# A hybrid decoder trunk with product-key experts: TensorE's weighted sum of v rows as 64x64 diagonal blocks, two slots at a time

## The chip, the cores and the metric

One Trainium2 chip, one core. The time is device microseconds for one execution of the whole program. Engines are called TensorE (PE; its weight loads PEld), VectorE (DVE), ScalarE (ACT), GpSimd (POOL) and SyncE (SP).

## The reference

Two layers on 512 tokens of width 1024, all in float32. Each layer first mixes tokens (norm, one input projection, a differential-attention group and a gated-linear-attention group, an output projection, residual). Then comes the part that takes most of the time, the retrieval of experts:

```python
def block(xb):                                   # 128 tokens
    q = (xb @ w_q).reshape(tb, 8, 2, 128)
    s = jnp.einsum('thcd,hckd->thck', q, sub_keys)
    top_s, top_i = lax.top_k(s, 16)
    ...
    u = u_tab[expert]                            # (128, 8, 16, 1024)
    act = jax.nn.gelu(jnp.einsum('td,thkd->thk', xb, u))
    w = gate * act
    return jnp.einsum('thk,thkd->td', w, v_tab[expert])
```

For each token, head and one of 16 picks, a row of 1024 floats comes from the table u and one from the table v: 2 layers x 512 tokens x 8 heads x 16 picks x 2 rows x 4 KB, 1.07 GB. The last line, the sum of v rows weighted by w, is what the change is about.

## The kernel before

**Units of work.** A tile is 128 tokens, one to a partition. A chunk is one head of one tile, 16 slots; a slot is one pick. There are 64 chunks, 1024 slots. For each slot GpSimd issues two indirect DMAs of 128 rows (`gather`, L464 to L471): a u row for each partition into `u_ring`, a v row into `v_ring`. Each ring has 6 buffers of 128x1024. GpSimd's order is fixed (L479 to L490): the u gather of slot s of chunk c+1, then the v gather of slot s of chunk c. A u gather waits until the slot six earlier is used (`u_used`), a v gather likewise (`v_used` if TensorE summed that slot, `v_added` if VectorE did).

**A slot's arithmetic.** VectorE multiplies the u rows with the tokens' h and sums over the row (`slot_u`, L986), a dot product for each partition. When the 16 dots of a chunk are there, ScalarE takes their gelu (`begin`, L659) and VectorE multiplies with the gates (L979): the 16 weights of a token. Then the v rows are summed. Of 16 slots VectorE takes slots 7 and 15 (`by_vector`), one scalar_tensor_tensor each onto `xs`, the residual (L996). TensorE takes the other 14: ScalarE writes a 128x128 diagonal matrix with the slot's weights (L669, from the identity, four buffers `diag`), and TensorE multiplies it with the v rows in two products of 128x512 that accumulate in PSUM (`slot_v`, L1257 to L1261). A float32 product stands in the trace as two MATMUL and two LDWEIGHTS instructions. `peer_acc` is 128x1024, two of eight PSUM banks. After the 8 chunks of a tile VectorE adds it to `xs` in one instruction (`add_tile`, L968 to L972), and TensorE's next tile waits for that (`peer_added`).

**Fronts.** All else (norms, projections, attention, the linear part, output projection, queries, top-k) is a front: 4 of them, each for 2 tiles of a layer. Each engine's program of a front is a generator that yields after each small part; 136 parts make a front, the last 40 of them routing. The first front runs alone up to part 101; from then on `interleave` (L338) puts parts between slots: each slot runs `slot_u` of the next chunk, then the front's parts that have come due (a front's parts spread over 256 slots, 10 ahead), then `slot_v`. So on TensorE the products of the next front (L1045, L1132, L1146, L1154) lie between the v slots, on VectorE its top-k and norms between the u products. From about 2772 us on there is no front left. Queues are in order on every engine: a wait holds all that stands behind it.

**Banks.** The six other PSUM banks carry the fronts' products. TensorE takes them in rotation, three for those that ScalarE empties (`fill_act`, L1009) and three for those that VectorE empties (`fill_dve`, L1015), and waits until the bank's last content is out. The order in which ScalarE and VectorE empty them is computed from the parts' positions (L136 to L153).

**Loads.** SyncE issues the weights, 2 MB at a time into two buffers, and the other inputs.

```python
for s in range(SLOTS):
    if c + 1 < CHUNKS:
        ...
        gather(u_rows, u_ring, U_RING, u_landed, c + 1, s)
    if c >= 0:
        ...
        pool.wait_ge(v_added if by_vector(old_s) else v_used, v_count(old_c, old_s))
        gather(v_rows, v_ring, V_RING, v_landed, c, s)
```

Of the kernel before, what the change touches and what calls it, by code (L numbers as in the profile page):

```python
# [22 lines left out]
P = 128  # L23
# [9 lines left out]
DIAGS = 4  # L33
ACT_BANKS = 3
DVE_BANKS = 3
V_EVERY = 8
LEAD = 10

# [15 lines left out]
def trunk(nc, x, attn_norm_w, w_in, q_norm_w, k_norm_w, lq1, lk1, lq2, lk2, diff_norm_w, gate_w2, gate_b,  # L54
# [40 lines left out]
    LR_AT = QK_AT + 4  # L95
    ATTN_AT = QK_FLIP_AT + HALF + 1
    ATTN_STEP = 5
    ATTN_STEPS = HALF * HEADS // 2
    GLA_AT = (LR_AT + 2, LR_AT + 16)
    FINISH_AT = (ATTN_AT + 14, ATTN_AT + 24)  # L100
# [35 lines left out]
    groups = [(2 * g, 0, "proj") for g in range(PROJ * HALF)] + [(LR_AT, 1, "lr")]  # L136
    groups += [(QK_FLIP_AT + i, 2, "qkT") for i in tiles for _ in range(2)]
    groups += [(ATTN_AT + ATTN_STEP * (s + 1), 3, "aT") for s in range(ATTN_STEPS) for _ in range(2)]
    groups += [(GLA_AT[i] + p, 4 + i, "gla") for i in tiles for p in (4, 4, 7)]
    groups += [(MIX_AT[i], 6, "mixT") for i in tiles for _ in range(2)]  # L140
    groups += [(STATS_AT[i] + 2, 7, "h2T") for i in tiles for _ in range(2)]
    groups += [(QUERY_AT, 0, "route"), (QUERY_AT + 2, 1, "route")]
    act_order = ["hT"] * 2 * HALF + [name for _, _, name in sorted(groups)] + ["route"] * (QS * QJ - 2)
# [34 lines left out]
    with ExitStack() as ctx:  # L178
        def sb(name, shape, dt=F32):
            return ctx.enter_context(nc.sbuf_tensor(name, shape, dt))  # L180
# [93 lines left out]
        wts = sb("wts", [P, 2, SLOTS])  # L274
        diag = sb("diag", [P, DIAGS, P])


        peer_acc = ctx.enter_context(nc.psum_tensor("peer_acc", [P, D], F32))
        act_bank = [ctx.enter_context(nc.psum_tensor(f"act_bank{i}", [P, 512], F32)) for i in range(ACT_BANKS)]
# [49 lines left out]
        def by_vector(s):  # L329

            return s % V_EVERY == V_EVERY - 1

# [96 lines left out]
        def _(pool):  # L429
# [10 lines left out]
            link(pool.memset(ident[:], 0.0))  # L440
            keep(ident[:], ALU.not_equal, 0, 1, [[-1, P]], 1.0)
            link(pool.memset(eps_c[:], EPS))
            link(pool.memset(one_c[:], 1.0))
# [50 lines left out]
        def _(act):  # L494
# [30 lines left out]
            def front(k):  # L525
# [11 lines left out]
                for p in range(MID_STEPS):  # L537
# [13 lines left out]
                    for _ in range(PRODUCT_PARTS[p]):  # L551
                        yield
                    if p == QUERY_AT + 3:
                        empty(scores[:, 0, 0])
                    if p == LR_AT + 1:
                        empty(lrT[0:RANK, :], HTOK, RANK)
                    i = p - QK_FLIP_AT - 1
                    if 0 <= i < HALF:
                        empty(qT[:, :, i * P:(i + 1) * P])
                        empty(kT[:, :, (t0 + i) * P:(t0 + i + 1) * P])  # L560
# [100 lines left out]
            def slot_v(c, s):  # L661
                if s == 0:
                    act.wait_ge(wts_ready, c + 1)
                if by_vector(s):
                    return
                n = v_count(c, s) - 1
                if n >= DIAGS:
                    act.wait_ge(v_used, n - DIAGS + 1)
                nc.scalar.activation(diag[:, n % DIAGS, :], ident[:], ACT.Copy,  # L669
                                     scale=wts[:, c % 2, s:s + 1]).then_inc(diag_ready, 1)  # L670
# [5 lines left out]
        def _(dve):  # L676
# [291 lines left out]
            def add_tile(tile):  # L968

                dve.wait_ge(v_used, (tile + 1) * PH * V_PE)  # L970
                v = xs[:, tile % TILES, :]
                tell(nc.vector.tensor_tensor(v, v, peer_acc[:], ALU.add), peer_added, "peer_added")  # L972

# [31 lines left out]
        def _(pe):  # L1005
# [45 lines left out]
            def front(k):  # L1051
# [8 lines left out]
                for p in range(MID_STEPS):  # L1060
# [26 lines left out]
                    if p == LR_AT:  # L1087
# [5 lines left out]
                        ins.then_inc(act_filled, 1)  # L1093
                    i = p - QK_FLIP_AT
                    if 0 <= i < HALF:
                        pe.wait_ge(qk_ready, k * HALF + i + 1)
                        for j in range(2):
                            flip([dqk[:, i, j * QH + h * P:j * QH + (h + 1) * P] for h in range(HEADS)])
# [3 lines left out]
                    for i in range(HALF):  # L1102
                        if p == MIX_AT[i]:
                            pe.wait_ge(mix_ready, k * HALF + i + 1)
                            flip_tile(mix[:, i, :])
                        if p == QUERY_AT + 2 and i == 0:
                            pe.wait_ge(keys_loaded, 16 * (l + 1))
                            pe.wait_ge(act_emptied, emptied(k, "route", 1))
                            score(0, 0)
# [136 lines left out]
            def slot_v(c, s):  # L1246
                if by_vector(s):
                    return
                tile, head = divmod(c, PH)
                n = c * SLOTS + s  # L1250
                e = head * TOPK + s
                last = head == PH - 1 and v_count(c, s) == (c + 1) * V_PE
                if e == 0 and tile > 0:
                    pe.wait_ge(peer_added, tile)
                pe.wait_ge(v_landed[n % V_RING], 16 * (n // V_RING + 1))
                pe.wait_ge(diag_ready, v_count(c, s))
                for j in range(D // 512):  # L1257
                    ins = nc.tensor.matmul(peer_acc[:, j * 512:(j + 1) * 512], diag[:, (v_count(c, s) - 1) % DIAGS, :],  # L1258
                                           v_ring[:, n % V_RING, j * 512:(j + 1) * 512],
                                           start=(e == 0), stop=last)  # L1260
                ins.then_inc(v_used, 1)  # L1261

# [31 lines left out]
```

## Time and profile before

| | |
|---|---|
| median of 3 runs | 3348.75 us (3347.01 to 3353.49) |
| span of the profiled execution | 3366.8 us (its own time beyond the span is not recorded) |
| instructions | 25897 |
| busy: TensorE, VectorE, ScalarE, GpSimd | 79%, 68%, 22%, 67% of the span |
| mean granted TensorE clock | 0.927 of full |
| first gather issued | 225.7 us |
| DMA | 1185 MB, mean 352 GB/s |

The profile is of one execution. Its time stands 18 us above the median of the runs, so differences are taken against it and then carried to the median. A wait row names the instruction that waited and what ended the wait; the time an engine is idle before an instruction costs something only if that engine is what others wait for. The DMA share of a stretch is the mean busy share of 16 DMA engines and can be a little over 1.

### The profile page before, as it was taken

How to read it: one execution, taken by the hardware profiler on the slowest of the kernel's cores; microseconds unless marked ns; L12 is line 12 of the kernel's file. 1: busy time of each engine (PE TensorE's matmuls, PEld its weight loads, DVE VectorE, ACT ScalarE, POOL GpSimd, SP SyncE). 2: the span in 40 equal slices, each digit the busy share in tenths (PEclk: the TensorE clock that was granted, in tenths of full speed). 3: DMA queues.
4: the chain of work that ended last, by engine and by line, in shares of the span. 5: the costliest groups of instructions: out<-in, count | busy, mean ns of one | idle time of the engine just before them, and what ended most of it. 6: DMA issues, size and time to landing. Idle time of an engine off the chain costs nothing.

```text
span 3366.8 us, 25897 instructions
## 1 busy us (share of the span) xinstructions
PE 2658.0 (79%) x7200; PEld 1257.8 (37%) x7200; DVE 2274.4 (68%) x4952; ACT 737.2 (22%) x1644; POOL 2267.3 (67%) x2074
## 2 busy tenths in 40 slices
PE   7866778998888778987887868998888776666667
PEld 3444333444354333433344423334435332222222
DVE  1559964579579984668659994568758995455443
ACT  2411121223221121223221121223322111111111
POOL 0025677777766777777776677777776676777776
PEclk9888899999998899999999889999999898988989
DMA  5248999999999999999999899999999999999998
GB/s 185 75 172 301 345 345 408 406 405 368 361 388 351 379 341 400 407 407 362 350 396 381 325 361 384 405 406 393 358 389 368 335 328 350 346 370 371 368 362 332
DMA packets 351442, 1185.41 MB, mean 352 GB/s; under 512 B 37666, under 2 KB 38212, under 8 KB 351044
## 3 DMA queue, kind: packets, MB, share of 16 engines
q0 software_dynamic: 294912, 1073.87, 84.2%
q1 hardware_dynamic: 56388, 109.88, 8.9%
q8 instruction: 60, 0.98, 0.1%
q14 instruction: 82, 0.67, 0.1%
HBM read 1181.52 MB, written 2.10 MB: 352 GB/s over the span
## 4 chain that ended last, share of the span: by engine, by line
POOL 27%; PE 23%; DVE 20%; issue 17%; DMA 11%; another core or an unknown queue 1%; ACT 1%; DVEq 0%; POOLq 0%; ACTq 0%
POOL v_ring L468 13%; POOL u_ring L468 13%; PE peer_acc L1258 12%; DMA v_ring<-in_peer_v,experts 8%; PE act_bank L1045 5%; DVE u_ring L986 4%; DMA u_ring<-in_peer_u,experts 4%; PE dve_bank L1045 2%; DVE work L752 2%; DVE work L741 1%; DVE work L749 1%; DVE work L738 1%; DVE work L931 1%; DVE work L933 1%
## 5 line engine op out<-in xcount | busy, mean ns | idle before, releaser
L1258 PE MATMUL peer_acc<-v_ring,diag 128*128 128x512 f32 x3584 | 1805.4, 645 | 647.1 <-DMA v_ring<-in_peer_v,experts 296.7
L986 DVE SCALAR_TENSOR_TENSOR u_ring<-u_ring,h 128x1024 f32<-128x1024 f32 x1024 | 1255.2, 1226 | 841.2 <-DMA u_ring<-in_peer_u,experts 730.1
L468 POOL DMA_INDIRECT v_ring<-in_peer_v,experts x1024 | 1146.9, 1120 | 524.3 <-issue 259.6
L468 POOL DMA_INDIRECT u_ring<-in_peer_u,experts x1024 | 1114.9, 1089 | 561.2 <-issue 308.9
L1258 PEld LDWEIGHTS peer_acc<-v_ring,diag 128*128 128x128 f32 x3584 | 688.5, 203 | 1647.7 <-issue 1009.4
L669 ACT ACTIVATE diag<-ident,wts 128x128 f32<-128x128 f32 x896 | 325.8, 397 | 1180.5 <-PE peer_acc L1258 580.9
L1045 PE MATMUL act_bank<-w_ring,hT 128*128 128x512 f32 x768 | 346.4, 598 | 0.7 <-ACT hT L508 0.7
L1045 PEld LDWEIGHTS act_bank<-w_ring,hT 128*128 128x128 f32 x768 | 147.5, 193 | 187.0 <-issue 185.6
L996 DVE SCALAR_TENSOR_TENSOR xs<-v_ring,wts,xs 128x1024 f32<-128x1024 f32 x128 | 164.5, 1285 | 49.5 <-DMA v_ring<-in_peer_v,experts 40.0
L1132 PE MATMUL act_bank<-hT,w_ring 128*128 128x256 f32 x768 | 175.6, 384 | 0.0
L1132 PEld LDWEIGHTS act_bank<-hT,w_ring 128*128 128x128 f32 x768 | 148.6, 194 | 39.4 <-issue 20.9
L508 ACT ACTIVATE work<-act_bank 128x512 f32<-128x512 f32 x72 | 43.0, 597 | 420.8 <-PE act_bank L1132 143.8
L659 ACT ACTIVATE acts<-dots 128x16 f32<-128x16 f32 x64 | 13.9, 216 | 491.6 <-issue 253.0
L1045 PE MATMUL dve_bank<-w_ring,hT 128*128 128x512 f32 x256 | 118.3, 609 | 2.5 <-ACT hT L508 1.7
L986 DVE DVE_READ_ACCUMULATOR u_ring<-u_ring,h 128x1 f32 x1024 | 84.1, 82 | 0.0
L1045 PEld LDWEIGHTS dve_bank<-w_ring,hT 128*128 128x128 f32 x256 | 50.5, 198 | 67.3 <-issue 65.1
L1146 PEld LDWEIGHTS act_bank<-hT,w_ring 128*128 128x128 f32 x512 | 59.7, 193 | 11.0 <-issue 10.0
L1146 PE MATMUL act_bank<-hT,w_ring 128*128 128x128 f32 x512 | 60.6, 276 | 3.2 <-issue 2.3
L508 ACT ACTIVATE hT<-act_bank 128x512 f32<-128x512 f32 (+3 forms) x80 | 39.0, 530 | 108.4 <-PE act_bank L1029 80.6
L659 ACT ACT_TABLE_LOAD x46 | 59.0, 1283 | 0.8
L617 ACT ACTIVATE work<-work,neg_max 128x128 f32<-128x128 f32 (+3 forms) x64 | 35.2, 551 | 52.3 <-DVE neg_max L829 38.1
L602 ACT ACTIVATE work<-work 128x32 f32<-128x32 f32 x32 | 7.4, 230 | 176.9 <-DVE work L950 125.2
(158 smaller groups left out, 1540.0 us busy)
## 6 DMA issues: line engine op xcount, KB each, us to landing
w_ring<-in_w_in SPq DMA_DIRECT2D x24, 2048.0 KB
w_ring<-in_peer_w_q SPq DMA_DIRECT2D x16, 2048.0 KB
w_ring<-in_w_out SPq DMA_DIRECT2D x8, 2048.0 KB
u_ring<-in_peer_u,experts POOLq DMA_INDIRECT x1024
v_ring<-in_peer_v,experts POOLq DMA_INDIRECT x1024
xs<-in_x SPq DMA_DIRECT2D x4, 512.0 KB, 7.2
keysT<-in_peer_sub_keys SPq DMA_DIRECT2D x2, 1024.0 KB
out<-xs SPq DMA_DIRECT2D x4, 512.0 KB
```

The costliest lines, as they stand in the source:

```text
L468: pool.indirect_dma_start(ring[:, n % depth, :], None, table, bass.IndirectOffsetOnAxis(ap=experts[:, tile % TILES, e:e + 1], axis=0),).th ...
L508: nc.scalar.activation(to, b[0:rows, 0:cols], ACT.Copy).then_inc(act_emptied, 1)
L617: ins = nc.scalar.activation(probs[:, m, 0:keys], probs[:, m, 0:keys], ACT.Exp, bias=neg_max[:, m:m + 1], accum_out=row_sum[:, m:m + 1])
L659: nc.scalar.activation(acts[:, c % 2, :], dots[:, c % 2, :], ACT.Gelu).then_inc(act_ready, 1)
L669: nc.scalar.activation(diag[:, n % DIAGS, :], ident[:], ACT.Copy, scale=wts[:, c % 2, s:s + 1]).then_inc(diag_ready, 1)
L752: ins = nc.vector.max_index(index[:, g, 8:16], tops[:, g, 8:16], values[:, g, :])
L986: tell(nc.vector.scalar_tensor_tensor(out=row, in0=row, scalar=1.0, in1=h2[:, tile % TILES, :], op0=ALU.mult, op1=ALU.mult, accum_out=dots ...
L996: tell(nc.vector.scalar_tensor_tensor(out=v, in0=v_ring[:, n % V_RING, :], scalar=wts[:, c % 2, s:s + 1], in1=v, op0=ALU.mult, op1=ALU.add ...
L1045: ins = nc.tensor.matmul(b[:], hT[:, c, i * P:(i + 1) * P], w[:, c, :], start=(c == 0), stop=(c == KC - 1))
L1132: ins = nc.tensor.matmul(b[:, s * HTOK:(s + 1) * HTOK], w[:, c, part * P:(part + 1) * P], hT[:, c, :], start=(c == 0), stop=(c == KC - 1))
L1146: ins = nc.tensor.matmul(b[:, g * P:(g + 1) * P], w[:, c, g * P:(g + 1) * P], hT[:, c, i * P:(i + 1) * P], start=(c == 0), stop=(c == KC - 1))
L1258: ins = nc.tensor.matmul(peer_acc[:, j * 512:(j + 1) * 512], diag[:, (v_count(c, s) - 1) % DIAGS, :], v_ring[:, n % V_RING, j * 512:(j + 1 ...
```

## The change

The v sum of TensorE takes its slots in pairs: within a chunk (0,1), (2,3), (4,5), (6,8), (9,10), (11,12), (13,14). At the second slot of a pair it waits for both v rows and both diagonals and then issues eight products, four for each half row of 512 columns, each with 64 partitions of contraction and a 64x64 block. The first slot's upper and lower halves of partitions go to their own output partitions, the second slot's go to the other half's, so that the four blocks lie on the four quadrants of the array. Products of the upper input partitions accumulate in one pair of banks (`peer_acc[:, 0]`), those of the lower in another (`peer_acc[:, 1]`). `v_used` rises by 2 after the pair.

ScalarE writes diagonals of 128x64 (`fold`, two identities of 64x64 one above the other, which GpSimd copies at the start). VectorE's add at the end of a tile is four instructions of 64x1024. `peer_acc` takes four banks, so the fronts have two and two instead of three and three. Some parts of a front move, so that no more than two banks are wanted at a time: the second tile's q/k flips come two parts after the first's instead of one, attention starts one part later and with it the output projection and what follows, the linear part two parts (first tile) and one part (second tile) later, the second query product's score one part earlier. A front has 137 parts instead of 136.

```diff
-ACT_BANKS = 3
-DVE_BANKS = 3
+ACT_BANKS = 2
+DVE_BANKS = 2
 V_EVERY = 8
+SIDE = 64
...
-    ATTN_AT = QK_FLIP_AT + HALF + 1
+    ATTN_AT = QK_FLIP_AT + 2 * HALF
...
-    GLA_AT = (LR_AT + 2, LR_AT + 16)
+    GLA_AT = (LR_AT + 4, LR_AT + 17)
...
-    groups += [(QK_FLIP_AT + i, 2, "qkT") for i in tiles for _ in range(2)]
+    groups += [(QK_FLIP_AT + 2 * i, 2, "qkT") for i in tiles for _ in range(2)]
...
-        diag = sb("diag", [P, DIAGS, P])
+        diag = sb("diag", [P, DIAGS, SIDE])
+        fold = sb("fold", [P, SIDE])
-        peer_acc = ctx.enter_context(nc.psum_tensor("peer_acc", [P, D], F32))
+        peer_acc = ctx.enter_context(nc.psum_tensor("peer_acc", [P, 2, D], F32))
...
+            for r in (0, SIDE):
+                link(pool.tensor_copy(fold[r:r + SIDE, :], ident[r:r + SIDE, r:r + SIDE]))
...
-                nc.scalar.activation(diag[:, n % DIAGS, :], ident[:], ACT.Copy,
+                nc.scalar.activation(diag[:, n % DIAGS, :], fold[:], ACT.Copy,
...
-                v = xs[:, tile % TILES, :]
-                tell(nc.vector.tensor_tensor(v, v, peer_acc[:], ALU.add), peer_added, "peer_added")
+                for r in range(2):
+                    v = xs[r * SIDE:(r + 1) * SIDE, tile % TILES, :]
+                    for turn in range(2):
+                        rows = slice((r ^ turn) * SIDE, ((r ^ turn) + 1) * SIDE)
+                        ins = nc.vector.tensor_tensor(v, v, peer_acc[rows, r, :], ALU.add)
+                        if r + turn < 2:
+                            link(ins)
+                        else:
+                            tell(ins, peer_added, "peer_added")
...
             def slot_v(c, s):
-                if by_vector(s):
+                count = v_count(c, s)
+                if by_vector(s) or count % 2:
                     return
                 tile, head = divmod(c, PH)
...
+                before = s - 2 if by_vector(s - 1) else s - 1
+                first = head == 0 and before == 0
+                last = count == (tile + 1) * PH * V_PE
+                if first and tile > 0:
                     pe.wait_ge(peer_added, tile)
-                pe.wait_ge(v_landed[n % V_RING], 16 * (n // V_RING + 1))
-                pe.wait_ge(diag_ready, v_count(c, s))
+                for one in (before, s):
+                    n = c * SLOTS + one
+                    pe.wait_ge(v_landed[n % V_RING], 16 * (n // V_RING + 1))
+                pe.wait_ge(diag_ready, count)
                 for j in range(D // 512):
...
-                ins.then_inc(v_used, 1)
+                    for turn, one in enumerate((before, s)):
+                        n, d = c * SLOTS + one, v_count(c, one) - 1
+                        for r in range(2):
+                            rows = slice(r * SIDE, (r + 1) * SIDE)
+                            to = slice((r ^ turn) * SIDE, ((r ^ turn) + 1) * SIDE)
+                            ins = nc.tensor.matmul(peer_acc[to, r, j * 512:(j + 1) * 512], diag[rows, d % DIAGS, :],
+                                                   v_ring[rows, n % V_RING, j * 512:(j + 1) * 512],
+                                                   start=first, stop=last)
+                ins.then_inc(v_used, 2)
```

## Rows read from the trace of the kernel before

**Rows 1.** The page: busy totals of the engines, and the gathers' DMA queue.

```profile
PE 2658.0 (79%) x7200; PEld 1257.8 (37%) x7200; DVE 2274.4 (68%) x4952; ACT 737.2 (22%) x1644; POOL 2267.3 (67%) x2074
...
q0 software_dynamic: 294912, 1073.87, 84.2%
```

**Rows 2.** Table of stretches; columns: stretch, length, busy us (instructions) of each engine, clock, DMA.

```profile
252.00:420.00 168.00, 118.55 (x348) 65.90 (x348) 160.00 (x507) 28.36 (x66) 99.94 (x91) 0.86 0.89 323
420.00:504.00 84.00, 61.79 (x144) 26.88 (x144) 57.63 (x123) 23.82 (x49) 62.35 (x57) 0.92 0.95 343
504.00:756.00 252.00, 224.30 (x571) 97.15 (x572) 153.66 (x245) 57.56 (x132) 183.82 (x172) 0.99 1.03 406
...
2016.00:2268.00 252.00, 230.51 (x556) 97.91 (x555) 139.32 (x221) 53.30 (x120) 186.27 (x174) 0.99 1.02 397
2268.00:2604.00 336.00, 285.12 (x907) 145.76 (x906) 250.92 (x487) 95.06 (x208) 246.14 (x221) 0.95 0.99 377
2604.00:2772.00 168.00, 122.85 (x348) 64.31 (x347) 158.72 (x473) 28.58 (x65) 115.68 (x103) 0.90 0.92 331
2772.00:3360.00 588.00, 395.21 (x733) 144.70 (x733) 289.23 (x465) 73.12 (x199) 431.99 (x401) 0.90 0.96 361
```

**Rows 3.** VectorE's longest wait, 1764 to 2016: us, times, longest.

```profile
DVE u_ring L986 <- DMA u_ring<-in_peer_u,experts: 3.9, 2, 2.5
```

**Rows 4.** The page's groups of gather issues, and one from the tail's timeline.

```profile
L468 POOL DMA_INDIRECT v_ring<-in_peer_v,experts x1024 | 1146.9, 1120 | 524.3 <-issue 259.6
L468 POOL DMA_INDIRECT u_ring<-in_peer_u,experts x1024 | 1114.9, 1089 | 561.2 <-issue 308.9
...
3001.24 0.94 POOL L468 DMA_INDIRECT u_ring<-in_peer_u,experts  x1 [0.30 <-issue]
```

**Rows 5.** Waits: whole run (two rows), then 252:420, 2604:2772, 504:756, 2016:2268, 2772:3360.

```profile
POOL v_ring L468 <- PE peer_acc L1258: 194.8, 158, 7.6
...
PEld dve_bank L1177 <- DVE work L826: 9.3, 12, 1.3
...
POOL v_ring L468 <- PE peer_acc L1258: 21.3, 9, 7.6
...
POOL v_ring L468 <- PE peer_acc L1258: 18.2, 10, 4.0
...
POOL v_ring L468 <- PE peer_acc L1258: 13.7, 15, 3.1
...
POOL v_ring L468 <- PE peer_acc L1258: 13.5, 15, 3.2
...
POOL v_ring L468 <- PE peer_acc L1258: 18.0, 26, 4.6
```

**Rows 6.** v sum on TensorE: two pieces of the chain, one of the timeline.

```profile
1410.40 6.87 PE peer_acc L1258 x16
...
444.88 3.69 PE peer_acc L1258 x4
...
3005.79 1.98 PE L1258 MATMUL peer_acc<-v_ring,diag 128*128 128x512 f32 x4 [0.57 <-DMA v_ring<-in_peer_v,experts]
```

**Rows 7.** TensorE's timeline at products of half height and half width.

```profile
756.70 1.13 PE L1177 MATMUL dve_bank<-kT,qT 64*128 64x512 f32 x4
...
1593.95 0.50 PE L1235 MATMUL dve_bank<-work,a_intra 128*128 128x128 f32 x3
...
1594.38 1.09 PE L1241 MATMUL dve_bank<-state,h 128*64 128x256 f32 x8
```

**Rows 8.** VectorE's instructions on 64 partitions: ns min/median/max.

```profile
L888 DVE SCALAR_TENSOR_TENSOR state<-state,decay,dve_bank x64: 337/347/355, 118.6 to 2389.0; 64x128 f32<-64x128 f32 x64
```

**Rows 9.** Timeline of the last chunk: a gather issue, VectorE's last v product, the add.

```profile
3341.74 0.94 POOL L468 DMA_INDIRECT v_ring<-in_peer_v,experts  x1 [0.78 <-PE peer_acc L1258]
...
3360.04 1.28 DVE L996 SCALAR_TENSOR_TENSOR xs<-v_ring,wts,xs 128x1024 f32<-128x1024 f32 x1 [11.36 <-DMA v_ring<-in_peer_v,experts]
3362.18 1.22 DVE L972 TENSOR_TENSOR xs<-xs,peer_acc 128x1024 f32<-128x1024 f32 x1 [0.85 <-PE peer_acc L1258]
```

More of the change, by code:

```diff
@@ L141, in trunk @@
     groups += [(STATS_AT[i] + 2, 7, "h2T") for i in tiles for _ in range(2)]
-    groups += [(QUERY_AT, 0, "route"), (QUERY_AT + 2, 1, "route")]
+    groups += [(QUERY_AT, 0, "route"), (QUERY_AT + 1, 1, "route")]
     act_order = ["hT"] * 2 * HALF + [name for _, _, name in sorted(groups)] + ["route"] * (QS * QJ - 2)
@@ L552, in front @@
                         yield
-                    if p == QUERY_AT + 3:
+                    if p == QUERY_AT + 2:
                         empty(scores[:, 0, 0])
@@ L556, in front @@
                         empty(lrT[0:RANK, :], HTOK, RANK)
-                    i = p - QK_FLIP_AT - 1
-                    if 0 <= i < HALF:
+                    i, off = divmod(p - QK_FLIP_AT - 1, 2)
+                    if off == 0 and 0 <= i < HALF:
                         empty(qT[:, :, i * P:(i + 1) * P])
@@ L1093, in front @@
                         ins.then_inc(act_filled, 1)
-                    i = p - QK_FLIP_AT
-                    if 0 <= i < HALF:
+                    i, off = divmod(p - QK_FLIP_AT, 2)
+                    if off == 0 and 0 <= i < HALF:
                         pe.wait_ge(qk_ready, k * HALF + i + 1)
@@ L1105, in front @@
                             flip_tile(mix[:, i, :])
-                        if p == QUERY_AT + 2 and i == 0:
+                        if p == QUERY_AT + 1 and i == 0:
                             pe.wait_ge(keys_loaded, 16 * (l + 1))
@@ L1246, in slot_v @@
             def slot_v(c, s):
-                if by_vector(s):
+                count = v_count(c, s)
+                if by_vector(s) or count % 2:
                     return
                 tile, head = divmod(c, PH)
[L1250 to L1253, printed above, removed]
+                before = s - 2 if by_vector(s - 1) else s - 1
+                first = head == 0 and before == 0
+                last = count == (tile + 1) * PH * V_PE
+                if first and tile > 0:
                     pe.wait_ge(peer_added, tile)
-                pe.wait_ge(v_landed[n % V_RING], 16 * (n // V_RING + 1))
-                pe.wait_ge(diag_ready, v_count(c, s))
+                for one in (before, s):
+                    n = c * SLOTS + one
+                    pe.wait_ge(v_landed[n % V_RING], 16 * (n // V_RING + 1))
+                pe.wait_ge(diag_ready, count)
                 for j in range(D // 512):
-                    ins = nc.tensor.matmul(peer_acc[:, j * 512:(j + 1) * 512], diag[:, (v_count(c, s) - 1) % DIAGS, :],
-                                           v_ring[:, n % V_RING, j * 512:(j + 1) * 512],
-                                           start=(e == 0), stop=last)
-                ins.then_inc(v_used, 1)
+                    for turn, one in enumerate((before, s)):
[7 more added lines that the diff above has]
+                ins.then_inc(v_used, 2)
             interleave(front, lambda c, s: None, slot_v, lambda c: None)
```

## The prediction

> **What bounds the kernel now.** I read the page's parts 1, 3 and 5 first, then a table of stretches, then the waits of the engine that issues the gathers, then single stretches of the timeline.
>
> The totals [rows 1] show three engines between 67% and 79% and no engine at its end, while the gathers alone fill 84.2% of the sixteen DMA engines over the whole span, the start included, where hardly any run. So the average says "DMA, nearly", and the average is not enough. The table [rows 2] divides the span into kinds of stretch. I tell them apart like this:
>
> - Start, 0 to 252: the first front alone. No v sum runs there.
> - At the DMA's end: 504 to 756, 1260 to 1512, 2016 to 2268 (the first and last are shown), share 1.02 to 1.03 and 397 to 406 GB/s. 756 us. Nothing on TensorE can move these while every byte stays.
> - At VectorE's end: 252 to 420, 1008 to 1176, 1764 to 2016, 2604 to 2772. VectorE is busy 160.0 of 168 us in the first and 158.7 of 168 in the last, 708.5 of 756 us in the four, 94%, and in the third it waits for u data for 3.9 us of 252 [rows 2, 3]; the rest is its own semaphore turns. Also TensorE-independent.
> - The rest: what else lies between 420 and 2604, five stretches from 420 to 504 to 2268 to 2604 (these two are shown), 1008 us, share 0.94 to 0.99, by length 0.98. There is slack to 1.03.
> - The tail, 2772 to 3360: no front. 401 gathers in 588 us, 2.93 us for a slot (a u and a v gather). One gather issue takes 0.94 us with 0.30 us between issues, so 2.48 us for two at best; over the run the two kinds mean 1.120 and 1.089 us [rows 4]: 1.12 + 1.09 + 0.60 = 2.81 us. So the tail is paced by GpSimd's issue, not by TensorE, which is busy 395 of 588 us.
>
> What TensorE does to this is seen where GpSimd waits for it: a v gather may not start before the slot six earlier is used. That is 194.8 us in 158 waits over the whole run [rows 5]: 42.8 us in the three DMA stretches (13.7 in the first, 13.5 in the last), 86.9 us in the four VectorE stretches (21.3 and 18.2), 18.0 us in the tail, so 47.1 us in the rest.
>
> **The change, part by part.**
>
> *The matmuls.* Before, a v slot is two 128x512 products, each two MATMUL instructions. Sixteen instructions (four slots) without a gap take 6.87 us, so 0.43 us each and 3.43 us for two slots; a slot that starts from idle takes 1.98 us [rows 6]. After, a pair is eight products of 64x64 blocks, sixteen instructions of the same 512 columns, on four quadrants. If the four run side by side, a quadrant has four instructions in a row: 4 x 0.43 = 1.72 us for the pair, half. Do they? No row has four quadrants, but both halves of the question have rows. Products on the two row halves: four instructions of 64x512 take 1.13 us, where four full ones take 1.98 [rows 6, 7]. Products on the two column halves with different moving data in the same rows: eight instructions of 256 columns take 1.09 us, where one after another at 0.21 us (half of 0.43) they would take over 8 x 0.21 = 1.7 us [rows 7]. Both are two-fold, with the second instruction of each product standing between in the program. I take four-fold in place: 1.72 us.
>
> The Trainium skill speaks against it. "TensorE: Matmul & The Clock Gate", Part 3 on packing, says that matmuls start and end strictly in program order, and that weight loads overlap only where the row group differs. By it each product's second instruction would hold back the next quadrant's first, the pair would cost eight strides of 0.43, 3.43 us as now, and the sum below would lose its gain. The rows on both halves contradict it for these shapes: with strict order the row halves would take three strides and a tail of 1.98 - 4 x 0.43 = 0.26 us, 1.55 us instead of 1.13, and the column halves at least 7 x 0.21 = 1.5 us instead of 1.09. What is left of the rule is in the first rival, whose price comes from rows.
>
> *Changes of array shape.* Between a front's full products and a pair the shape changes twice. One such change is visible: the three last full 128-column instructions of a group start at 1593.95 and end at 1594.45, so at 0.11 us a stride the last starts at 1594.17; the first 64-column one starts at 1594.38, 0.21 us later [rows 7]. 0.1 us more than a stride, twice for each of 448 pairs at most: 90 us of TensorE, against 448 x 1.72 = 770 us saved. TensorE goes from 2658 us busy to about 1980. It is backlogged in the fronts today, so its lag behind the data shrinks; but this is worth only what somebody waits for it.
>
> *Release in pairs.* The first slot of a pair is released with the second: one slot later, 2.93 us, and two slots for (6, 8), where VectorE owns slot 7. Against it stands 1.7 us less work. Where v is behind, the net is about +1.2 us for the first and -1.7 us for the second. ScalarE may prepare the next pair's diagonals while a pair runs, as four buffers are two pairs; a diagonal of 64 columns instead of 128 is no longer than today's.
>
> *By stretch.* DMA stretches: 0. VectorE stretches: their GpSimd waits are effects of a late VectorE, and data waits of VectorE are all that could go: -3. Rest: bounded by the share, 1008 x (1 - 0.98/1.03) = 49 us, and by GpSimd's 47.1 us; I take half, -24, because the paired release keeps a part. Tail: of 18.0 us I take -10; some 3.5 us of these are certain, the last chunk, where the gathers are held to TensorE's pace (0.78 instead of 0.30 us before an issue, six alike and one of 0.96) [rows 9].
>
> *Folding the partial sums.* The add at a tile's end was one instruction of 1.22 us on 128x1024; it becomes four of 64x1024. An instruction's time follows columns, not partitions: 64x128 takes 0.34 us [rows 8]. So 4 x 1.22 plus links, +3.7 us at each of 8 tiles. Three of them (1066, 1851, 2634) lie in VectorE stretches and cost in full: +11. Of the other five, four are covered by gathers in flight (bounds 0 and +3.7 each; I take 0, as VectorE is busy only some 0.6 of those stretches [rows 2] and six u buffers stand ahead of it), and the last is bare: +3.7, less 0.9 us because VectorE's last v product ends at 3361.32, 0.9 us before the add, which waits for TensorE [rows 9]: +3.
>
> *Fewer banks, parts moved.* Two banks instead of three for each evacuator, the q/k flips two parts apart, attention one part later, the linear part two and one later; a front has 137 parts instead of 136, on the same 256 slots. TensorE waits for a bank of VectorE's 9.3 us in 12 waits today [rows 5]; twice this is the upper bound, 0 the lower, a small gain by luck of order not excluded (-3). Most lies under the bounds above; the start, where the front is alone, takes +2. The extra weight loads (7168 instead of 3584, half as wide) are shadowed by 0.43 us strides; if not, 1.72 grows. Two more GpSimd copies at the start: under 1 us, before weights land.
>
> Sum: -3 - 24 - 10 + 11 + 3 + 2 = **-21 us**. The profiled execution's span is 3366.8 us, 18 us above the median of 3348.75; its own time beyond the span is not given, so I carry the difference: 3348.75 - 21 = 3328 us. About 0.2%, 7 us, is what a measurement here can tell.
>
> **Rivals.**
>
> *No overlap of the four (0.08).* Strict order, or a limit once both halves are used together. TensorE keeps 3.43 us a pair, pays the 90 us of shape changes, and releases later; I let the 195 us of GpSimd's waits grow by a half, 97 us, add the 90 us, and count the third that lies in the rest and the tail today ((47.1 + 18.0) / 194.8), 62 us, and the 14 us of the adds: 3348.75 + 76 = 3425. For: no row with four. Against: both pairs of halves.
>
> *The paired release turns into the wait (0.20): slower.* Place: GpSimd before a v gather. Let half of the 158 waits of today be on a first slot. If TensorE there is not late by its own work but by landing or diagonals, nothing of the 1.7 us comes back and each waits 2.93 us longer: 79 x 2.93 = 231 us at most; the four-fold sum halves those with backlog. It decides where GpSimd comes to the buffer less than a slot spacing after its release. With 100 us more of waits, a third of them in the rest and the tail, and 14 us of adds: 3348.75 + 47 = 3396; with half of that, 3372. For: those waits exist, up to 7.6 us [rows 5]. Against: in the tail GpSimd waits 18 us in all, with its buffer wanted six slots of 2.93 us after the gather, 17.6 us.
>
> *The clock gives it back (0.17): no change.* The granted clock is 0.99 where TensorE is busy 89% and 0.86 to 0.90 where it is busy 67 to 73% [rows 2]; less busy, it may be granted half speed more often. At 1.2 GHz a slot takes 3.69 us (the piece at 444.88, whose stride is twice the usual one, which I read as the lower of the clock's two levels) instead of 1.98 [rows 6], and a pair about what two warm slots take today. Time near 3345.
>
> *It gives all that the bounds leave (part of the forecast's case).* -49 - 18 - 3: 3279.
>
> **Numbers.** Forecast 0.55, its own range 3279 to 3340; no change 0.17; slower 0.28. The range goes from 3278 to 3385, leaving out the first rival and the worse half of the second.
>
> **What would show it.** A pair's sixteen instructions in about 1.9 us and TensorE's busy total near 1980 us; GpSimd's waits for TensorE under 100 us; gathers a little denser in the rest and the tail; VectorE and DMA stretches as long as now; four adds near 1.22 us each. Wrong would be: a pair in 3.4 us or more; GpSimd's waits above 200 us; a clock under 0.8 in the fronts.

## The result and the profile after

Before 3348.75 us (3347.01 to 3353.49), after **3494.06 us** (3489.55 to 3498.21): ratio 1.041, interval 1.038 to 1.045. Slower by 145 us where 21 us less was forecast, and outside the range. The spans of the profiled executions are 3366.8 and 3496.4 us, +130.

The page of the changed kernel, to be read against [rows 1, 4]:

```profile
PE 2197.7 (63%) x10784; PEld 916.1 (26%) x10784; DVE 2306.2 (66%) x4976; ACT 668.8 (19%) x1644; POOL 2265.8 (65%) x2076
...
q0 software_dynamic: 294912, 1073.87, 82.1%
...
L1278 PE MATMUL peer_acc<-v_ring,diag 64*64 64x512 f32 x7168 | 1216.3, 808 | 1110.5 <-issue 629.8
```

TensorE's work did shrink, by 460 us. VectorE got 32 us more (the adds), ScalarE 68 us less, GpSimd the same; what fills the longer span is waiting. TensorE's timeline at pairs shows that the change does what it says:

```profile
1406.34 1.95 PE L1278 MATMUL peer_acc<-v_ring,diag 64*64 64x512 f32 x16 [0.72 <-issue]
1411.41 3.51 PE L1278 MATMUL peer_acc<-v_ring,diag 64*64 64x512 f32 x16 [3.12 <-issue]
1414.85 7.13 PE L1056 MATMUL act_bank<-w_ring,hT 128*128 128x512 f32 x16
...
3100.99 3.52 PE L1278 MATMUL peer_acc<-v_ring,diag 64*64 64x512 f32 x16 [3.39 <-issue]
```

Sixteen instructions of 512 columns in 1.95 us, as long as one slot's four took from idle [rows 6]: all four quadrants run side by side. The second and fourth rows are the same sixteen at the lower level of the clock; the third is a front's product. The table of stretches (columns as in [rows 2]) has the clock at 0.90 in the first row, a stretch where TensorE is busy 59.70 of 84 us, and at 0.67 in the next two: a stretch where the fronts leave TensorE little to do (33.23 of 84 us), and most of the tail. The last row is the one pair at 3101, where 0.58 is granted, near the lower level of 1.2 GHz.

```profile
588.00:672.00 84.00, 59.70 (x277) 21.28 (x278) 46.83 (x73) 16.10 (x40) 60.18 (x56) 0.90 1.02 393
...
2016.00:2100.00 84.00, 33.23 (x188) 9.48 (x192) 80.38 (x223) 20.66 (x47) 59.19 (x52) 0.67 0.94 347
2940.00:3444.00 504.00, 244.52 (x1212) 62.15 (x1216) 248.71 (x384) 45.77 (x163) 378.82 (x346) 0.67 0.98 362
3100.90:3104.80 3.90, 3.52 (x16) 0.90 (x16) 1.27 (x4) 0.00 (x0) 2.99 (x4) 0.58 1.02 402
```

The tail keeps its pace at that clock: 346 gathers in 504 us, 2.91 us for a slot, against 2.93 before. So the loss is elsewhere. Counting gathers in the trace, slot 128's v gather starts at 689 us instead of 663, slot 192's at 897 instead of 851, slot 640's at 2321 instead of 2227; slot 768's is the one below, at 2733.87 instead of 2615.02, and from there on the gap stays at 113 to 124 us until the last chunk. Nearly all of it is lost while fronts run.

```profile
2733.87 0.94 POOL L472 DMA_INDIRECT v_ring<-in_peer_v,experts  x1 [0.30 <-issue]
```

The same count divides the loss among the prediction's kinds of stretch, each taken from slot to slot. Of the 128 us by which the last v gather is late, 12 are there at the first, 50 come in the three DMA stretches, for which the prediction had 0, 48 in the rest, 7 in the four VectorE stretches and 10 in the tail. The first DMA stretch, before and after, by the same slots:

```profile
504.40:758.20 253.80, 226.50 (x581) 98.27 (x582) 155.43 (x247) 58.43 (x134) 185.32 (x172) 0.99 1.03 406
...
522.30:798.20 275.90, 191.17 (x872) 70.11 (x876) 163.54 (x256) 55.47 (x138) 184.86 (x172) 0.84 0.98 377
```

The DMA engines, which were full, are no longer: 0.98 instead of 1.03. What held the gathers back, GpSimd's and TensorE's waits tell (waits of the whole run: us, times, longest; the first answers to [rows 5]):

```profile
POOL v_ring L472 <- PE peer_acc L1278: 291.9, 127, 12.2
POOL u_ring L472 <- DVE experts L969: 249.8, 4, 228.0
```

```profile
PE dve_bank L1230 <- DVE work L830: 26.4, 4, 9.7
PE dve_bank L1238 <- DVE a_intra L880: 19.7, 4, 5.8
PE dve_bank L1188 <- DVE work L830: 17.9, 5, 5.6
...
PE act_bank L1056 <- ACT qT L512: 16.7, 5, 7.0
```

GpSimd waits for TensorE 97 us more than before, in fewer and longer waits (2.3 us each instead of 1.2). It is idle 129 us more in all, as much as the span grew: beside the 97, 16 for the experts (10 of them at the start), 18 in v waits whose end the profile puts down to no engine, and small sums both ways. And TensorE waits for banks, which hardly happened before. The release in pairs has its own picture in GpSimd's timeline of the last chunk, against 0.78 us before each issue in [rows 9]:

```profile
3465.54 0.94 POOL L472 DMA_INDIRECT v_ring<-in_peer_v,experts  x1 [3.50 <-PE peer_acc L1278]
3466.79 0.94 POOL L472 DMA_INDIRECT v_ring<-in_peer_v,experts  x1 [0.30 <-issue]
3468.03 0.94 POOL L472 DMA_INDIRECT v_ring<-in_peer_v,experts  x1 [0.30 <-issue]
...
3477.93 0.94 POOL L472 DMA_INDIRECT v_ring<-in_peer_v,experts  x1 [5.22 <-PE peer_acc L1278]
```

Buffers come back in bursts, and before a burst the queue stands for 3.5 and 5.2 us.

### The profile page after: what moved, and what is told of

Same layout as the page of the kernel before. It is cut to its first block, busy times and chain, and to the rows that moved or that the text cites. A ratio compares the mean times of both kernels' runs of the same rounds, so it can differ in the third digit from the quotient of the medians.

```text
span 3496.4 us, 32651 instructions
## 1 busy us (share of the span) xinstructions
PE 2197.7 (63%) x10784; PEld 916.1 (26%) x10784; DVE 2306.2 (66%) x4976; ACT 668.8 (19%) x1644; POOL 2265.8 (65%) x2076
## 4 chain that ended last, share of the span: by engine, by line
POOL 24%; DVE 22%; issue 20%; PE 19%; DMA 11%; ACT 2%; another core or an unknown queue 1%; DVEq 0%; POOLq 0%
POOL v_ring L472 13%; POOL u_ring L472 12%; PE peer_acc L1278 9%; DMA v_ring<-in_peer_v,experts 7%; PE act_bank L1056 6%; DMA u_ring<-in_peer_u,experts 5%; DVE u_ring L997 5%; DVE work L756 2%; DVE work L745 1%; PE dve_bank L1056 1%; DVE xs L1007 1%; DVE work L742 1%; DVE work L753 1%; DVE work L937 1%; DVE work L935 1%
## 5 line engine op out<-in xcount | busy, mean ns | idle before, releaser
L1278 PE MATMUL peer_acc<-v_ring,diag 64*64 64x512 f32 x7168 | 1216.3, 808 | 1110.5 <-issue 629.8
L472 POOL DMA_INDIRECT v_ring<-in_peer_v,experts x1024 | 1136.7, 1110 | 629.7 <-PE peer_acc L1278 291.9
L1278 PEld LDWEIGHTS peer_acc<-v_ring,diag 64*64 64x64 f32 x7168 | 321.6, 168 | 1850.5 <-issue 1827.5
L673 ACT ACTIVATE diag<-fold,wts 128x64 f32<-128x64 f32 x896 | 263.8, 340 | 1543.2 <-PE peer_acc L1278 969.8
L1056 PE MATMUL act_bank<-w_ring,hT 128*128 128x512 f32 x768 | 375.8, 640 | 35.1 <-ACT qT L512 16.7
L1143 PE MATMUL act_bank<-hT,w_ring 128*128 128x256 f32 x768 | 185.6, 399 | 0.0
L1188 PE MATMUL dve_bank<-kT,qT 64*128 64x128 f32 (+3 forms) x128 | 42.8, 620 | 19.6 <-DVE work L830 17.9
L979 DVE TENSOR_TENSOR xs<-xs,peer_acc 64x1024 f32<-64x1024 f32 x32 | 39.0, 1219 | 19.5 <-PE peer_acc L1278 18.5
```

Of the source, the lines that this page charges most:

```text
L472: pool.indirect_dma_start(ring[:, n % depth, :], None, table, bass.IndirectOffsetOnAxis(ap=experts[:, tile % TILES, e:e + 1], axis=0),).th ...
L673: nc.scalar.activation(diag[:, n % DIAGS, :], fold[:], ACT.Copy, scale=wts[:, c % 2, s:s + 1]).then_inc(diag_ready, 1)
L1056: ins = nc.tensor.matmul(b[:], hT[:, c, i * P:(i + 1) * P], w[:, c, :], start=(c == 0), stop=(c == KC - 1))
L1143: ins = nc.tensor.matmul(b[:, s * HTOK:(s + 1) * HTOK], w[:, c, part * P:(part + 1) * P], hT[:, c, :], start=(c == 0), stop=(c == KC - 1))
L1188: nc.tensor.matmul(b[:, 0:keys], qT[rows, h, i * P:(i + 1) * P], kT[rows, h, 0:keys], start=True, stop=True).then_inc(dve_filled, 1)
L1278: ins = nc.tensor.matmul(peer_acc[to, r, j * 512:(j + 1) * 512], diag[rows, d % DIAGS, :], v_ring[rows, n % V_RING, j * 512:(j + 1) * 512] ...
```

## The experiments

Theories: **B**, two banks instead of three stop TensorE in a front with v products queued behind; **P**, the common wait and release of two slots hold GpSimd; **C**, the clock that falls gives back the halved work. Every ratio is against the kernel before on the same chip, whose median was 3356, 3368, 3359 and 3358 us in the four sets.

**e1_banks.** The kernel before with the fronts' part of the change alone.

```diff
-ACT_BANKS = 3
-DVE_BANKS = 3
+ACT_BANKS = 2
+DVE_BANKS = 2
-    ATTN_AT = QK_FLIP_AT + HALF + 1
+    ATTN_AT = QK_FLIP_AT + 2 * HALF
...
```

> The kernel before with the fronts' part of the change alone: two banks instead of three for each evacuator and the parts moved; v sum as before (one slot at a time, full array, peer_acc two banks). Theory B (banks: TensorE is stopped in a front until VectorE or ScalarE has emptied a bank, and the v products queued behind it release their buffers late): 3400 or more, most of the 130 us of span, GpSimd's waits for TensorE above 240 us, start later by some 10 us. Theory P (release in pairs) and theory C (clock): within 15 us of 3349.

Measured 3411.9 us, 1.017 (1.015 to 1.019). B is true and has 1.7% of the 4.1%. Its waits:

```profile
POOL v_ring L468 <- PE peer_acc L1258: 244.9, 174, 9.4
...
POOL u_ring L468 <- DVE experts L965: 253.7, 4, 233.6
...
PE dve_bank L1219 <- DVE work L826: 21.5, 4, 9.0
...
PE dve_bank L1227 <- DVE a_intra L876: 12.1, 4, 4.0
PE act_bank L1045 <- ACT qT L508: 11.9, 3, 7.4
```

The first row grew by 50 us. The second is the start: GpSimd's one long wait for the first experts is 233.6 us, where it is 218.0 before.

**e2_pairs.** The kernel before with paired slots, all on the full array.

```diff
-                if by_vector(s):
+                count = v_count(c, s)
+                if by_vector(s) or count % 2:
                     return
...
+                for one in (before, s):
+                    n = c * SLOTS + one
+                    pe.wait_ge(v_landed[n % V_RING], 16 * (n // V_RING + 1))
+                pe.wait_ge(diag_ready, count)
+                for one in (before, s):
+                    ...
-                ins.then_inc(v_used, 1)
+                ins.then_inc(v_used, 2)
```

> The kernel before with its slots taken in pairs: TensorE waits for both v rows and both diagonals, then issues the four full 128x512 products of two slots, and v_used rises by two; three and three banks, parts unmoved. Theory P: at least as slow as the changed kernel, since nothing of the halved work is had: 3450 or more, GpSimd's waits for TensorE above 290 us. Theory B and theory C: 3349 to 3375.

Measured 3450.4 us, 1.029 (1.026 to 1.032): the largest part. GpSimd's wait is as in the changed kernel:

```profile
POOL v_ring L468 <- PE peer_acc L1262: 290.3, 125, 10.7
```

**e3_filler.** The changed kernel with products of zeros behind each pair.

```diff
+FILL = 2
...
                 ins.then_inc(v_used, 2)
+                for j in range(FILL if not last else 0):
+                    for turn in range(2):
+                        for r in range(2):
+                            ...
+                            nc.tensor.matmul(peer_acc[to, r, 0:512], none[rows, :], causal[rows, 0:512],
+                                             start=False, stop=False)
```

> The changed kernel with eight products of a 64x64 block of zeros after each pair (behind the signal that releases the pair), so that TensorE is about as busy as before and its clock is kept; the sums are the same, as zeros are added. Theory C (the clock fell from 0.927 to 0.789 and gives back the halved work): granted clock about 0.92 again and the time back to 3350 to 3420. Theory B and theory P: 3490 or slower, up to 3550, as the filler's time comes on top.

Measured 3532.1 us, 1.053 (1.049 to 1.057). The whole run's row of stretches has the clock at 0.91, and TensorE 2843.54 us busy:

```profile
0.00:3535.00 3535.00, 2843.54 (x17824) 1201.46 (x17824) 2305.08 (x4976) 671.72 (x1644) 2245.28 (x2077) 0.91 0.91 336
```

The clock came back and the time did not; it grew by another 38 us. C had forecast 3350 to 3420. By itself this run leaves room for a loss by the clock hidden under the filler's own work, but e1_banks above and e2_pairs show 1.7% and 2.9% of loss with the clock at 0.90 to 0.91, without any quadrants. C as the main cause of the loss is out.

**e4_single.** The changed kernel with each slot for itself on two quadrants, odd and even slots on different ones.

```diff
-                for one in (before, s):
-                    n = c * SLOTS + one
-                    pe.wait_ge(v_landed[n % V_RING], 16 * (n // V_RING + 1))
+                turn = (count - 1) % 2
+                pe.wait_ge(v_landed[n % V_RING], 16 * (n // V_RING + 1))
...
-                ins.then_inc(v_used, 2)
+                ins.then_inc(v_used, 1)
```

> The changed kernel with each slot for itself: a slot's four 64x64 products go to two quadrants, odd slots to the other two, and each slot waits for its own row and diagonal and releases by one. Two slots that follow each other without a front's product between them may still overlap. Theory P: most of the loss comes back, 3400 or less. Theory B: 3470 to 3500, little comes back. Theory C: 3450 to 3500; a slot has 1.7 us warm and 3.4 us cold as before.

Measured 3436.0 us, 1.025 (1.023 to 1.028). That is 1.6%, some 53 us, under the changed kernel: less than P said, and more than B or C. What is left is about what the banks (1.7%) and the adds (0.6%, e6_add4 below) cost.

**e5_moves.** e1_banks with three and three banks.

> The kernel before with the parts of the fronts moved as in the change (flips two parts apart, attention one part later, the linear parts two and one later, the score one earlier), but with three and three banks. If the 55 us of e1_banks come from the count of banks: within 10 us of the kernel before. If they come from the moved parts: 3395 or more, and the first gather issued some 10 us later.

Measured 3382.6 us, 1.005 (1.003 to 1.007). Moved parts cost 0.5%, the count of banks the other 1.2%. The start is unmoved here (longest wait for experts 216.5 us), so its 15 us belong to the banks.

**e6_add4.** The kernel before with four adds at a tile's end.

```diff
-                tell(nc.vector.tensor_tensor(v, v, peer_acc[:], ALU.add), peer_added, "peer_added")
+                for r, op in ((0, ALU.add), (0, ALU.subtract), (0, ALU.add), (1, ALU.add)):
+                    rows = slice(64 * r, 64 * r + 64)
+                    ins = nc.vector.tensor_tensor(v[rows, :], v[rows, :], peer_acc[rows, :], op)
...
```

> The kernel before with four chained adds of 64x1024 at a tile's end instead of one of 128x1024 (one of them subtracts what the one before it added, so that the sum stays): the price of folding two partial sums. By the sum of the prediction: +14 us (3.7 us at each of three tile ends in VectorE's stretches and at the last). If tile ends are critical everywhere: 8 x 3.7 = +30 us. If buffers hide it: +4 us.

Measured 3387.2 us, 1.006 (1.0045 to 1.008): 20 us, between the 14 of the prediction and 30.

**e7_defer.** e2_pairs with waits and release for each slot.

```diff
-                for one in (before, s):
-                    n = c * SLOTS + one
-                    pe.wait_ge(v_landed[n % V_RING], 16 * (n // V_RING + 1))
-                pe.wait_ge(diag_ready, count)
                 for one in (before, s):
+                    ...
+                    pe.wait_ge(v_landed[n % V_RING], 16 * (n // V_RING + 1))
+                    pe.wait_ge(diag_ready, v_count(c, one))
...
+                    ins.then_inc(v_used, 1)
-                ins.then_inc(v_used, 2)
```

> As e2_pairs, but inside a pair each slot waits for its own row and diagonal and is released by one; only the place is kept, both slots behind the front's parts of the second. Theory R (it is the common wait and the common release that hold the first buffer): most of the 94 us of e2_pairs comes back, 3380 or less. Theory L (it is the place, one slot later in TensorE's queue and behind a front's product): 3420 or more.

Measured 3379.1 us, 1.003 (1.001 to 1.005). It keeps the first slot's place, late in TensorE's queue, and still gives back nine tenths of e2_pairs' loss. GpSimd's wait is nearly that of the kernel before:

```profile
POOL v_ring L468 <- PE peer_acc L1260: 197.7, 146, 11.1
```

So it is the common wait and common release together. Which of the two weighs more was not tried apart.

**e8_banks_pairs.** e1_banks and e2_pairs together: the changed kernel without quadrants and with one add.

> The changed kernel without its quadrants: two and two banks, moved parts, pairs with common wait and release, but four full 128x512 products and one add. If quadrants gain nothing here: within 15 us of the changed kernel, 3480 to 3510 (55 + 94 us over before). If the halved work saves what GpSimd waits: 3530 or more, slower than the changed kernel by 40 us. If banks and pairs hold the same time up only once: 3450.

Measured 3534.1 us, 1.050 (1.0485 to 1.052). 1.7 + 2.9 = 4.6, so the costs add, and a little more. The changed kernel, which has 0.6% of adds on top, stands at 4.1: the quadrants give back 5.0 + 0.6 - 4.1 = 1.5%, some 50 us. GpSimd's wait for TensorE grew by 361.3 - 194.8 = 167 us, and the profiled span by 158 us, from 3366.8 to 3524.9. The two are near each other, but not the same time: GpSimd's waits for the experts grew by 18 us as well, and its other waits for VectorE fell by 32.

```profile
POOL v_ring L468 <- PE peer_acc L1262: 361.3, 132, 9.9
```

**e9_diag8.** The changed kernel with `DIAGS = 8`.

> The changed kernel with eight diagonal buffers instead of four. v_used releases diagonals as well as v rows. If the paired release costs because ScalarE stands before a diagonal (969.8 us of such waits) and empties the fronts' banks late: 3460 or less, and TensorE's waits for banks shrink. If it costs through GpSimd's ring alone: within 10 us of the changed kernel (ratio 1.041 to the kernel before).

Measured 3484.5 us, 1.0385 (1.0355 to 1.042). The interval overlaps the changed kernel's, so the quarter per cent between them is not clear of noise. GpSimd's waits for TensorE are as before, 286.4 against 291.9 us. GpSimd's ring is the main way, and ScalarE's diagonals are not.

**e10_quad_defer.** e7_defer's waits and releases on the quadrants of the changed kernel.

```diff
-                for one in (before, s):
-                    n = c * SLOTS + one
-                    pe.wait_ge(v_landed[n % V_RING], 16 * (n // V_RING + 1))
-                pe.wait_ge(diag_ready, count)
-                for j in range(D // 512):
-                    for turn, one in enumerate((before, s)):
+                for turn, one in enumerate((before, s)):
+                    ...
+                    for j in range(D // 512):
...
+                    ins.then_inc(v_used, 1)
```

> The changed kernel with e7_defer's order inside a pair: the first slot's four quadrant products wait for its own row and diagonal and release by one, the second's likewise, so that they overlap fully where both are there. If the costs found so far add up (banks and moved parts +1.7%, add +0.6%, place +0.3%) and the quadrants give back what e8_banks_pairs shows against the changed kernel with its add (5.0 - 4.1 + 0.6 = 1.5%): ratio 1.011, about 3395. If the quadrants' gain was only in taking off waits that the pairs had made: 1.02 to 1.03.

Measured 3460.7 us, 1.0315 (1.0285 to 1.035): a miss. Without the common wait and release the quadrants gain nothing: 1.7 + 0.6 + 0.3 = 2.6% of costs would stand with no gain at all, and it is 3.2. The clock does not explain it: 0.88 here and 0.89 in e4_single, which shows no gain either, are near the 0.89 to 0.90 of e8_banks_pairs on the full array. A slot whose partner is not there runs on two quadrants and takes as long as on the full array (TensorE's timeline of this kernel, eight instructions of one slot with the full clock granted; compare 1.98 us in [rows 6]):

```profile
3051.05 1.93 PE L1275 MATMUL peer_acc<-v_ring,diag 64*64 64x512 f32 x8 [1.48 <-DMA v_ring<-in_peer_v,experts]
3053.66 1.93 PE L1275 MATMUL peer_acc<-v_ring,diag 64*64 64x512 f32 x8 [0.68 <-DMA v_ring<-in_peer_v,experts]
```

**e11_a3d2.** e1_banks with three banks for ScalarE, two for VectorE.

> The kernel before with moved parts, three banks for ScalarE and two for VectorE. Between e5_moves (ratio 1.005, three and three) and e1_banks (1.017, two and two). If it is VectorE's banks, whose waits grew most in the changed kernel (26.4, 22.8, 19.7 us): 1.014 or more. If ScalarE's: 1.008 or less.

Measured 3392.4 us, 1.010 (1.007 to 1.013): between. Of the banks' 1.2%, some 0.5% are VectorE's third bank and 0.7% ScalarE's, each within 0.3% or so; neither alone.

**e12_before57.** The kernel before with `U_RING = 5`, `V_RING = 7`.

> The kernel before with five u buffers and seven v buffers instead of six and six, in the same memory. GpSimd waits 194.8 us for a v buffer and 18.9 us for a u buffer. If a v buffer's release is the loss and the u side has room: 3320 to 3340, faster. If u buffers become the wait: slower by 10 us or more.

Measured 3358.8 us, 1.000 (0.999 to 1.002), neither. GpSimd's wait for a v buffer halves, from 194.8 us, and the one for a u buffer, 18.9 us before, takes its place:

```profile
POOL u_ring L468 <- DVE u_ring L986: 150.9, 81, 6.6
POOL v_ring L468 <- PE peer_acc L1258: 90.2, 123, 4.2
```

So a wait of GpSimd's is not yet a loss: 105 us of them went and the time stayed. A seventh v buffer was not tried with the pairs, where the waits for it are longer.

**e13_fill1.** e3_filler with `FILL = 1`.

> e3_filler with half the filler, four products of zeros after each pair: 0.86 us of TensorE's time at full clock, under what the quadrants save (1.72 us). If the low clock costs time in the fronts: the clock back near 0.88 to 0.91 for half the work added, and faster than the changed kernel by 10 us or more (ratio under 1.038). If it costs nothing, as the unchanged pace of the tail at 0.65 says: between the changed kernel (1.041) and e3_filler (1.053).

Measured 3504.7 us, 1.043 (1.040 to 1.0465), clock 0.853. Not faster than the changed kernel at any setting of the filler; a small cost of the low clock, hidden by the filler's own, is not excluded.

**e14_before_d8** and **e15_single8.** `DIAGS = 8` in the kernel before and in e4_single.

> The kernel before with eight diagonal buffers instead of four. ScalarE waits 580.9 us for TensorE before a diagonal; if banks are emptied late because of it, faster by 5 us or more, as e9_diag8 was against the changed kernel (1.0385 against 1.041); otherwise the same.

> e4_single with eight diagonal buffers: the best the quadrants can be here without the common wait. If ScalarE's place before a diagonal costs: 1.020 or less, against 1.0254 of e4_single. It cannot beat the kernel before if banks (+1.7%) and adds (+0.6%) are paid in full.

Measured 3360.6 us, 1.001 (0.999 to 1.003), and 3433.2 us, 1.022 (1.019 to 1.025). More diagonals do nothing before; in e4_single the intervals overlap. No version here beats the kernel before.

## Why the prediction was wrong

**The matmuls: right.** 1.95 us for a pair from idle, against "about 1.9". What the rows on both halves of the array showed, and not the rule of strict order, held for the four together. The first rival fell.

**TensorE's busy total: half right.** "about 1980" came out 2197.7. A pair from idle takes 1.95 us and not the 1.72 of the sum, up to 448 x 0.23 = 103 us; the rest is mostly the clock, 0.789 instead of 0.927, which also lengthened the fronts' products (640 instead of 598 ns in the largest group). The third rival named this. But the clock was not the cause of the loss: banks and pairs cost their 1.7%, 2.9% and together 5.0% (e1, e2, e8) on the full array with the clock at 0.89 to 0.91, and e3 and e13 brought back the clock and not the time.

**Release in pairs: the step that failed.** In the sum the paired release only "keeps a part" of the 49 us that the rest could give, so that 24 were taken, and the second rival priced it at 23 to 47 us, the adds included. Alone it measures 94 us (e2). Two errors made it small.

The first is the trade of 2.93 us of lateness against 1.7 us of work, which was to leave +1.2 us for the first slot of a pair and -1.7 us for the second. The traces give it directly, as the time from the start of a slot's v gather to the end of its products, mean over all pairs:

| us | first slot | second slot |
|---|---|---|
| before | 13.25 | 12.97 |
| e2_pairs | 16.21 | 12.54 |
| e7_defer | 13.57 | 12.60 |
| changed kernel | 15.72 | 11.99 |

So the first slot's buffer is held 2.5 us longer in the changed kernel, twice what was expected, and the second's is back 1.0 us earlier. The trade holds only where TensorE is late by its own work; elsewhere the first slot stays held until the second has landed and is summed. e7 keeps the place and drops the common wait and the common release, and the 94 us shrink to 11.

The second error is in which waits count. I took DMA and VectorE stretches as out of TensorE's reach and counted only the third of a new wait that lies in the rest and the tail. Time added and GpSimd's waits for TensorE added, by kind of stretch, against the kernel before (us, counted in the traces as in the section on the result; the start is left out):

| time / waits | DMA | rest | VectorE | tail |
|---|---|---|---|---|
| changed kernel | 50 / 49 | 48 / 32 | 7 / 13 | 10 / 4 |
| e2_pairs | 43 / 28 | 22 / 14 | 4 / 37 | 5 / 18 |
| e8_banks_pairs | 73 / 59 | 64 / 58 | -2 / 36 | 9 / 12 |
| e12_before57 | 0 / -10 | -11 / -29 | -3 / -78 | -11 / 13 |

For VectorE's stretches the prediction was right: 37 us of new waits there cost 4, and 78 us fewer (e12) gave back 3. For the DMA stretches it was wrong. That nothing on TensorE can make them shorter is a bound for gains, not for losses: their share fell, in the first from 1.03 to 0.98, and the time added is no less than the waits added, in all three of the kernels that lose. Late gathers that leave the DMA engines without work are the likely reason.

**Fewer banks: mis-sized.** +2 us, upper bound about 19; measured 55 us with the moved parts, 40 of them the banks. I bounded them by twice the bank waits of the kernel before, 9.3 us. But these waits are low because there are three banks; the next bank's wait is not in that row. And each stop holds the v products queued behind it: in e1 GpSimd's waits grew by 50 us, and TensorE's own waits for ScalarE and VectorE before products into the fronts' banks, summed over its waits list, from 43 to 106 us.

**The adds: near.** +14 against 20 us; one took 1.22 us on 64 partitions as on 128.

**The gain: right in size and wrong in kind.** 21 + 14 + 2 = 37 us were expected of the halved work; 50 are there (worked out by subtraction, e8 against the changed kernel), but e10 and e4 show that they only take back part of what the common wait and release cost. Without these there was no gain to have. That GpSimd, VectorE and the DMA engines set the pace there fits the stretches of [rows 2], but was not tried by itself. Two of the signs that the prediction had named as wrong are in the profile: GpSimd's waits above 200 us (291.9) and a clock under 0.8 in stretches of the fronts (0.67 in the one shown).

Altogether: 1.7 (banks and moves) + 2.9 (pairs) + 0.4 (both together) + 0.6 (adds) - 1.5 (quadrants) = 4.1%. The sum closes because the last term was got by subtraction; the others were measured, each within 0.2 to 0.3%.

## What to carry to other kernels

Before work on an engine is halved, ask what has to be held together for it: two slots that share a wait and a release cost a ring of six more (94 us) than the engine's work saved (50 us). A stretch in which the DMA engines are full admits no gain, but it takes a loss when gathers come late; in a stretch that VectorE fills, waits of the same size cost nothing. So the same wait row has different prices in different stretches. And the wait on a resource says nothing about the wait with one fewer: only a run with the resource taken away, which is a two-line edit, prices it.

## What was not expected of the hardware

Four products of 64x64 blocks run side by side in float32: sixteen instructions take 1.95 us, where four full ones take 1.98. Less TensorE work lowered the granted clock, from 0.927 to 0.789 over the run (0.853 and 0.911 with the two sizes of filler) and to 0.67 over the tail, where a pair then takes 3.5 us, nearly the 3.43 us of two full slots at the higher level; there it cost nothing. And one slot on two quadrants is no faster than on all of the array, so the packing pays only with both slots present.
